# Turned copies of x, positions and taps from the host in a three-block fp32 transformer kernel

## The reference

```python
for l in range(2):
    h = rms_norm(x, pre_g[l])
    p = split_columns(h @ w_in[l] + b_in[l])       # 14 groups of columns, 6992 in all
    # four mixers: stick-breaking, sparse (with compressed blocks), forgetting, latent attention
    # compress_blocks: silu((tokens[:, gather] + pos_emb).reshape(...) @ w1) @ w2
    # latent_attention: rms_norm(c_q) @ w_uq, rms_norm(c_kv) @ w_ukv
    x = x + rms_norm(concat(mixers * silu(gates)) @ w_out[l], post_g[l])
proj = rms_norm(x, norm1_g) @ w_in_2               # banded attentions and a causal conv of 31 taps
x = x + concat(...) @ w_out_2
h2 = rms_norm(x, norm2_g)
x = x + (silu(h2 @ w_gate) * (h2 @ w_up)) @ w_down
```

## Time and profile before

| what | value |
| --- | --- |
| median of the runs | 1979.77 us |
| span of the profiled execution, first to last instruction | 1977.6 us |
| median less span | 2.2 us |
| PE busy | 1963.8 us, 99% of the span |
| DVE, ACT, POOL busy | 58%, 48%, 4% |
| span less PE busy | 13.8 us |
| DMA, whole span | 360.74 MB, mean 182 GB/s |
| DMA in the first two fortieths of the span | 289 and 201 GB/s |

### The profile page before, as it was taken

The page is one execution under the profiler, slowest core; times in us unless marked ns, Lnnn a source line. Parts: engine busy times, 40 slices in busy tenths (PEclk is TensorE's granted clock), DMA queues, the critical chain, the costliest instruction groups (busy, mean ns, idle before and its releaser), DMA issues.

```text
span 1977.6 us, 27533 instructions
## 1 busy us (share of the span) xinstructions
PE 1963.8 (99%) x10170; PEld 1666.5 (84%) x10170; DVE 1145.0 (58%) x1352; ACT 945.6 (48%) x1256; POOL 80.1 (4%) x125
## 2 busy tenths in 40 slices
PE   9999999999999999999999999999999999999999
PEld 7898988887899998888778788888888888888887
DVE  6584555556666554655757986645454444444443
ACT  6355444444564554444655564544444444443342
POOL 4000000001200000000300100000000000000000
PEclk9999999999999999999999999999999999999999
DMA  8664555665755445666555435666666666656653
GB/s 289 201 221 125 165 163 164 191 197 158 251 178 193 145 145 150 194 197 187 168 171 161 143 133 181 193 191 191 191 188 184 190 191 189 189 180 214 205 203 128
DMA packets 188153, 360.74 MB, mean 182 GB/s; under 512 B 13202, under 2 KB 20417, under 8 KB 187793
## 3 DMA queue, kind: packets, MB, share of 16 engines
q1 hardware_dynamic: 183408, 346.15, 56.3%
q0 software_dynamic: 4640, 13.20, 2.4%
HBM read 357.20 MB, written 2.10 MB: 182 GB/s over the span
## 4 chain that ended last, share of the span: by engine, by line
PE 97%; DVE 1%; ACT 1%; DMA 0%; issue 0%; ACTq 0%; POOL 0%; DVEq 0%; SPq 0%; POOLq 0%
PE psum L627 26%; PE psum L629 25%; PE psum L628 25%; PE psum L635 3%; PE psum L638 3%; PE psum L637 3%; PE psum L1334 1%; PE psum L745 1%; PE psum L1110 1%; PE psum L759 1%; PE psum L734 1%; PE psum L891 0%; PE psum L1591 0%; PE psum L653 0%; PE psum L655 0%; PE psum L654 0%
## 5 line engine op out<-in xcount | busy, mean ns | idle before, releaser
L593 DVE TENSOR_TENSOR wl<-raw,wh 128x1024 fp32r<-128x1024 f32 (+1 forms) x655 | 775.4, 1196 | 663.2 <-ACT wh L585 656.0
L585 ACT ACTIVATE wh<-raw 128x1024 fp32r<-128x1024 f32 (+1 forms) x655 | 671.9, 1036 | 826.7 <-PE psum L629 681.8
L627 PE MATMUL psum<-wh,xh 128*128 128x512 f32 (+2 forms) x1584 | 615.5, 389 | 5.0 <-DVE xl L929 4.1
L629 PE MATMUL psum<-wh,xl 128*128 128x512 f32 (+2 forms) x1584 | 608.8, 384 | 0.0
L628 PE MATMUL psum<-wl,xh 128*128 128x512 f32 (+2 forms) x1584 | 608.6, 384 | 0.0
L627 PEld LDWEIGHTS psum<-wh,xh 128*128 128x128 f32 x1584 | 297.6, 188 | 67.0 <-DVE xl L929 7.1
L629 PEld LDWEIGHTS psum<-wh,xl 128*128 128x128 f32 x1584 | 297.5, 188 | 58.7
L628 PEld LDWEIGHTS psum<-wl,xh 128*128 128x128 f32 x1584 | 297.8, 188 | 56.7
L635 PE MATMUL psum<-xh,wh 128*128 128x256 f32 x512 | 146.1, 285 | 0.0
L638 PE MATMUL psum<-xl,wh 128*128 128x256 f32 x512 | 144.9, 283 | 0.0
L637 PE MATMUL psum<-xh,wl 128*128 128x256 f32 x512 | 144.9, 283 | 0.0
(11 more groups left out here) (422 smaller groups left out, 1600.8 us busy)
## 6 DMA issues: line engine op xcount, KB each, us to landing
raw<-in_w_in_dram SPq DMA_DIRECT2D x263, 512.0 KB, 4.3
raw<-in_w_out_dram SPq DMA_DIRECT2D x96, 512.0 KB, 3.9
raw<-in_w_gate_dram SPq DMA_DIRECT2D x88, 512.0 KB, 3.6
raw<-in_w_up_dram SPq DMA_DIRECT2D x88, 512.0 KB, 3.6
raw<-in_w_down_dram SPq DMA_DIRECT2D x80, 512.0 KB, 3.6
cmp_raw<-in_cmp_w_dram SPq DMA_DIRECT2D x16, 512.0 KB, 4.4
raw<-in_w_small_dram SPq DMA_DIRECT2D x16, 336.0 KB, 3.1
bias<-in_b_in_dram POOLq DMA_DIRECT2D x18, 256.0 KB, 4.1
```

Of the source, the lines that this page charges most:

```text
L585: act.activation(wh[:, n % SPLIT_SLOTS, 0:k, 0:unit.n], buffer[:, 0:k, 0:unit.n], ACT.Copy).then_inc(hi_done, 1)
L593: dve.tensor_tensor(out=wl[:, n % SPLIT_SLOTS, 0:k, 0:unit.n], in0=buffer[:, 0:k, 0:unit.n], in1=wh[:, n % SPLIT_SLOTS, 0:k, 0:unit.n].bit ...
L627: pe.matmul(o, ah_[:, kt, tok], hi_w, start=first, stop=False)
L629: ins = pe.matmul(o, al_[:, kt, tok], hi_w, start=False, stop=last)
```

## The change

The host also passes x with columns in partitions (`x_turned`, 128 x 16 x 256), the positions turned (`pos_turned`) and the taps of the conv turned (`conv_w_turned`).

- In layer 0, `xt` takes the turned x (in the place of `ml`); ACT and DVE make the operand from it directly, so the 32 transposes of x in layer 0 go. SP loads `xt` in pieces of two row tiles ahead of each of the first units, and x by tokens (two DMAs of 1 MB) behind raw7 and raw8. The squares of x stand behind the high splits of units 9 and 10, where they stood ahead of those of 6 and 7.
- The gains, the identity and one piece of `xt` are issued by ACT's queue at the very start, where the identity was issued by SP and the gains by POOL.
- DVE takes the operand ahead of the split of each unit, ACT too. The first unit's products are written out in another order, with seven idle products ahead where there were eight and six.
- Positions come by one DMA straight to `posT`; PE's two small transposes and DVE's copy go, in both layers. Taps come straight to `conv_wT`; PE's four small transposes and ACT's copy go in the third block.
- POOL starts its masks when the last piece of `xt` has landed, and issues `w_uq` when seven parts of the operand are done.
- `_out_high` signals of the third block share one semaphore; no instruction moves by that.

```diff
@@ act_first, layer 0
-                act.wait_ge(raw_first, 16)
+                act.wait_ge(xt_first, 16)
+                x_high(0, xt[:, 0, :]).then_inc(first_x_high, 1)
+                act.wait_ge(raw_first, 16)
                 act.activation(wh[:, 0, 0, :], raw[:, 0, 0, :], ACT.Copy).then_inc(first_high, 1)
-                act.wait_ge(s(name + "_turned"), 1)
-                x_high(0, all_banks[:, x_column(0):x_column(0) + T])
-                x_high(1, all_banks[:, x_column(1):x_column(1) + T]).then_inc(s(name + "_high"), 1)
+                act.wait_ge(*xt_signal(0))
+                x_high(1, xt[:, 1, :]).then_inc(s(name + "_high"), 1)
...
-                if n >= 6:
-                    act_norm(name, scratch, updates, n - 6)
+                act_operand(place, name, n)
                 split_high(place, n, units[n])
-                act_operand(place, name, n)
@@ dve_first, layer 0
-                for n in range(2, PARTS):
+                for n in range(1, PARTS):
+                    operand(n)
                     split(n)
-                    operand(n)
@@ SP
+            def load_xt(k0, k1, loaded):
+                sp.dma_start(xt[:, k0:k1, :], d["x_turned"][:, k0:k1, :]).then_inc(loaded, 16)
+            def load_x(tb):
+                sp.dma_start(x[:, tb, :], d["x"][0, tb * P:(tb + 1) * P, :]).then_inc(x_loaded[tb], 16)
...
+                    if l == 0 and n < PARTS:
+                        load_xt(2 * n, 2 * n + 2, xt_loaded[n % XT_SEMS])
+                    load_unit(sp, place, n, layer_units[n], layer_src(l))
+                    if l == 0 and n in (PARTS - 1, PARTS):
+                        load_x(n - PARTS + 1)
@@ POOL
-            load(norm_g, d["norm_gains"][0, :, :], norm_g_loaded)
-            pool.wait_ge(x_loaded[BLOCKS - 1], 16)
+            pool.wait_ge(*xt_signal(PARTS - 1))
...
-                pool.wait_ge(s("pre_turned"), part_signal(place, l, PARTS - 1))
+                if l:
+                    pool.wait_ge(s("pre_turned"), part_turned(place, PARTS - 1))
+                else:
+                    pool.wait_ge(s("pre_operand"), PARTS - 1)
...
-                load(pos_in[0:CMP_LEN, 0, :], mat("nsa_cmp_pos_k"), layer_loads)
-                load(pos_in[0:CMP_LEN, 1, :], mat("nsa_cmp_pos_v"), layer_loads)
+                load(posT[:, :, :], d["pos_turned"][bass.ds(l, 1), :, :, :].rearrange("a p i n -> (a p) i n"),
+                     layer_loads)
@@ PE, first unit and the two small turnings
-            pe_idle_products(8, False)
-            block_0 = pe_turn_block("pre", 0, 0)
-            next(block_0)
-            pe_idle_products(6, False)
+            pe_idle_products(7, False)
+            pe.wait_ge(first_operand, 1)
+            pe.wait_ge(first_high, 1)
...
-                    pe.wait_ge(layer_loads, 16 * LAYER_LOADS * place.once)
-                    for i in range(2):
-                        ins = pe.transpose(st[:, 1024 + 32 * i:1024 + 32 * (i + 1)], pos_in[0:CMP_LEN, i, :],
-                                           ident[0:CMP_LEN, 0:CMP_LEN])
...
-            def turn_conv_weights():
@@ ACT
+            act.dma_start(norm_g, d["norm_gains"][0, :, :]).then_inc(ident_loaded, 16)
+            act.dma_start(ident[:, :], d["c_ident"]).then_inc(ident_loaded, 16)
+            act.dma_start(xt[:, 1:2, :], d["x_turned"][:, 1:2, :]).then_inc(xt_loaded[0], 16)
...
+                if l == 0:
+                    after_unit.update({PARTS + 1 + tb: lambda tb=tb: act_norm("pre", xn, 0, tb) for tb in range(TB)})
```

More of the change, by code:

```diff
@@ L874, in wait_x @@
         def wait_x(eng, name, updates, b):
[L875 to L878, removed]
+            eng.wait_ge(x_ready, BLOCKS * (updates - 1) + b + 1)
         def act_norm(name, scratch, updates, tb):
             act = nc.scalar
-            for b in range(BLOCKS if updates <= LAYERS else 1):
-                wait_x(act, name, updates, b)
+            if updates == 0:
+                act.wait_ge(x_loaded[tb], 16)
+            else:
+                for b in range(BLOCKS if updates <= LAYERS else 1):
+                    wait_x(act, name, updates, b)
             act.activation(scratch[:, :], x[:, tb, :], ACT.Square, accum_out=x_sums[:, tb:tb + 1])
@@ L901, in pe_turn_block @@
         def pe_turn_block(name, updates, b):
[L903 to L907, removed]
+            wait_x(nc.tensor, name, updates, b)
+            for ins in turn_x(range(4 * b, 4 * b + 4), all_banks, x_column(4 * b)):
                 ins.then_inc(s(name + "_turned"), 1)
[L909 to L912, removed]
         def pe_turn_rows(name, updates, tb):
@@ L940, in rows_signal, with xt_signal, turned_before, part_turned @@
             return parts_before(place) + 2 * tb + part + 1
+        def xt_signal(part):
+            return xt_loaded[part % XT_SEMS], 16 * (part // XT_SEMS + 1)
+        def turned_before(place):
+            return (PARTS + 2) * max(place.once - 2, 0)
+        def part_turned(place, part):
+            return turned_before(place) + part + 3
+        def rows_turned(place, tb, part):
+            return turned_before(place) + 2 * tb + part + 1
         def rows_column(kt, tb):
@@ L945, in act_rows_operand @@
         def act_rows_operand(place, name, tb, part):
-            nc.scalar.wait_ge(s(name + "_turned"), rows_signal(place, tb, part))
+            nc.scalar.wait_ge(s(name + "_turned"), rows_turned(place, tb, part))
             for kt in (2 * part, 2 * part + 1):
@@ L1074, in pe_first_operand @@
             if n < PARTS:
-                for b in {3: (2,), 5: (3,)}.get(n, ()):
-                    for _ in pe_turn_block(name, updates, b):
-                        pass
+                if updates and n in (3, 5):
+                    pe_turn_block(name, updates, {3: 2, 5: 3}[n])
                 nc.tensor.wait_ge(s(name + "_operand"), part_signal(place, updates, n))
@@ L1082, in pe_first_units @@
             pe = nc.tensor
-            pe_idle_products(8, False)
-            block_0 = pe_turn_block("pre", 0, 0)
-            next(block_0)
-            pe_idle_products(6, False)
[L1088 to L1098, removed]
-                    pe.wait_ge(lo_done, RAW_SLOTS + 2)
-                else:
-                    for _ in pe_turn_block("pre", 0, 1):
-                        pass
-            multiply(place, 0, units[0], pieces=first)
-            multiply(place, 1, units[1], pieces=second)
+            pe_idle_products(7, False)
+            pe.wait_ge(first_operand, 1)
+            pe.wait_ge(first_high, 1)
+            for tb in range(TB):
+                tok, o = slice(tb * P, (tb + 1) * P), acc[0][:, tb, :]
+                pe.matmul(o, xh[:, 0, tok], wh[:, 0, 0, :], start=True, stop=False)
+                pe.matmul(o, xl[:, 0, tok], wh[:, 0, 0, :], start=False, stop=False)
+            pe.wait_ge(first_low, 1)
+            for tb in range(TB):
+                pe.matmul(acc[0][:, tb, :], xh[:, 0, tb * P:(tb + 1) * P], wl[:, 0, 0, :], start=False, stop=False)
+            pe.wait_ge(s("pre_operand"), 1)
+            pe.wait_ge(lo_done, RAW_SLOTS + 1)
+            for tb in range(TB):
+                tok, o = slice(tb * P, (tb + 1) * P), acc[0][:, tb, :]
+                pe.matmul(o, xh[:, 1, tok], wh[:, 0, 1, :], start=False, stop=False)
+                pe.matmul(o, xh[:, 1, tok], wl[:, 0, 1, :], start=False, stop=False)
+                ins = pe.matmul(o, xl[:, 1, tok], wh[:, 0, 1, :], start=False, stop=False)
+            ins.then_inc(unit_used, 1)
+            pe_first_operand(place, "pre", 1, 0)
+            multiply(place, 1, units[1])
         def pe_turn_mix(o, bank):
@@ L1281, in _ @@
             load(log_count[:, :], d["c_log_count"], block2_loads)
-            pool.wait_ge(s("first2_turned"), part_signal(place, LAYERS, PARTS - 1))
-            load(conv_raw[0:TAPS, :], d["conv_w_2"][0, :, :], block2_loads)
+            pool.wait_ge(s("first2_turned"), part_turned(place, PARTS - 1))
+            load(conv_wT[:, :, :], d["conv_w_turned"], block2_loads)
             pool_norm(place, "first2")
```

96 lines of the change are left out of this document (46 added, 50 removed).

## The result

The changed kernel takes 1984.09 us (median of 15 runs, 1983.26 to 1986.59), the kernel before 1979.84 in the same session: 4.25 us slower, ratio 1.0022, 95% interval 1.0015 to 1.0029. The prediction was 1984.1.

What follows compares the result with a forecast made beforehand. The chain from layer 0's loads to unit 12 was taken to bind: +4.6 us there less 0.35 for the taps gives +4.3, a span of 1981.9, and with 2.2 around it 1984.1 us; range 1979.4 to 1986.4.

Steps and rivals of the forecast that it cites:

- What bounds it: Layer 0: the chain from the layer's loads to unit 12 has only 0.26 us of slack; shifts carry to layer's end.
- What goes from PE: Layer 0: 32 transposes go, unit 1 starts at 11.55, not 12.35; PE alone would gain 4.2 us by stage 2.
- Landing of the loads: Layer 0: POOL's last load lands at 40.3, 4.9 us late; unit 12 +4.6 us.
- served nearly in order of issue: DMA engines: weights issued before w_uq, and the second x at 5.2 us, count as ahead of POOL's loads.
- the two units that I counted: Layer 0 weights: raw11 and raw12 now issued ahead of w_uq, adding 1.3 us each to the landing.
- PE stands idle at units 9 or 10 for raw: Layer 0: a sign, named beforehand, that the forecast is wrong.
- add nothing: ACT, layer 0: squares of x behind unit 10's split cost nothing; they and POOL's factors are done by 38.
- PE's wait: Layer 0: PE idle some 8 us ahead of unit 11, then without a gap from unit 12 at about 52.
- Taps: Third block: turning the taps on the host spares PE four small transposes, a plain gain of 0.35 us.
- Faster: Rival, chance 0.05: chain does not bind, PE's 4.2 us and the taps' 0.35 come through; 1975.2 us.
- Worse: Rival, chance 0.10: raw10 and x land behind POOL's loads, or raw12 and raw13 stand ahead; +5.5 to +7, 1985.3 to 1987.
- The queue yields: Rival, chance 0.28: POOL's loads share the engines with SP's, landing 36.5 to 38.5; +0.5 to +2.5, 1980.3 to 1982.3.

Runs made afterwards that it cites:

- e1: Changed kernel without the two loads of x by tokens (2 MB), POOL filling x with a constant; 1983.76 us, ratio to the kernel before 1.0019.
- e5: Changed kernel without the second x, and with POOL's masks begun at the fourth piece of xt; 1982.62 us, ratio to the kernel before 1.0013.
- e8: Kernel before with only the positions and the taps turned on the host; 1979.24 us, ratio 0.9996.
- e9: Changed kernel without the second x, POOL's masks from the fourth piece of xt, both squares of x behind unit 8; 1978.56 us.
- e12: Changed kernel, all loads kept; layer 0: squares of x behind unit 8, latents read out one split earlier, w_uq's two splits later; 1978.62 us.
- e6: Changed kernel with both squares of x behind unit 8, and SP holding raw 11 and later weights until the layer's loads have landed; 1981.89 us.
- e11: Kernel before plus two more 1 MB loads of x into a free place, behind raw 7 and raw 8; 1985.52 us, ratio 1.0028.
- e10: Changed kernel with squares of x behind unit 8, and w_uq's two splits moved behind the latents' work and a later unit, both layers; 1981.12 us.
- e3: Changed kernel with both squares of x behind the high split of unit 8; 1983.74 us, ratio to the kernel before 1.0020.

## Why the prediction was right, point by point

- *The number.* That it fits to the hundredth is luck. The traced span grew by 3.8 and not by 4.3. In every run 1.7 to 1.9 us lie around the span; the 2.2 that I took from before, and the 2.7 of the changed kernel, hold also by how much the traced execution was quicker than the median, and that made up the half microsecond.
- *What bounds it.* Right: the chain from the layer's loads sets unit 12. Unit 12 +4.34 (forecast +4.6), then no idle time of PE from 55 to 460, and most of the shift stays: +4.04 at PE's longest wait in the seam to layer 1 (486.89 for 482.85).
- *What goes from PE.* Unit 1 at 11.07, forecast 11.55: raw 1 came 0.8 earlier than I took it. Worth nothing, as said.
- *Landing of the loads.* Forecast 40.3, measured 39.9; w_uq issued at 28.05, forecast 28.4, where my own terms (19.6 + 8.5) give 28.1. The number is right, the sum behind it is not sound. "Ahead of it in the DMA engines there is now x a second time: 5.2 us" would have e1 land at about 35; it landed at 39.5, since the ring of weights fills the place. The step that fails is "served nearly in order of issue". Two errors offset: taking x away moved this landing by 0.5 and not by 5.2, and more weights shared its time than the two units that I counted. x had landed at 28.3, just as w_uq was issued; it had pushed back raw 9, 10, 11 and 12, which landed at 32.6, 35.5, 39.5 and 40.9, around posT at 39.9.
- *Raw 9.* I priced x against POOL's loads and not against raw 9, which stands behind it in SP's own queue. I named "PE stands idle at units 9 or 10 for raw" as a sign against me; it came (2.04 us). It stayed hidden since PE had over 4 us in hand, but it held ACT too: the squares ended at 38.73, 1.27 us before L1812. That the squares "add nothing" was nearly false, and e5 shows where it becomes so.
- *PE's wait.* Forecast some 8 us ahead of unit 11; measured 2.04 + 3.84. The rest, 2 us, went into slower products: a stretch at half clock from 36.14 to 39.48, by which units 9 and 10 took 7.4 us and not 5.5. I did not foresee it, nor the second stretch, in unit 11 itself (last section).
- *Small parts.* Taps -0.27 (forecast -0.35: the first product there still starts 0.40 behind the last, not 0.228). Layer 1: nothing, as forecast. Positions in layer 0: in e8 0.38 for unit 12, hidden in the changed kernel.
- *The rivals.* "Faster" (1975.2) had the condition that the last load lands before 31.2. That is not enough: in e9 posT landed at 31.3 (issued at 22.47, 8.8 us), yet L1812 began at 34.99, behind two squares and two splits on ACT, and the time was 1978.6. Nor do the loads alone decide, as e12 shows. "Worse" has a wrong sum at its lower end: squares at 42.7 are 5.2 late, and less the 0.26 of slack and the 0.35 of the taps that is +4.6, inside the forecast, and not +5.5. "The queue yields" is half true as a mechanism (rows of both queues are served together) and wrong in its time.

What stays open: why raw 10 lands at 35.5 in the changed kernel and at 38.1 in e6 with fewer bytes behind it, and whether e8, e9 and e12 are faster than the kernel before. The medians say 0.7 to 1.3 us, the ratios' intervals reach past 1, and in the traces unit 12 of e9 and e12 starts no earlier than before (48.07 and 47.72 for 47.56).

## What to carry to other kernels

When the DMA engines are full, a load that you take away need not give its bytes back at the load that you care about: here a prefetch ring filled the place (in e1 0.5 us came back, of the 5.2 that 2 MB take at 402 GB/s). One that you add can cost all of them (5.1 us in e11). Ask which loads are queued at that moment, on all queues. And before paying with bytes for a faster engine, look for work in the late chain that stands ahead of the wait and need not: here four moves on ACT and DVE gave 5.5 us with every load as it was. Where several waits end within 2 us of each other, as here, single edits can show next to nothing though all of them together show the whole.

## What the hardware showed beyond that

After PE's waits of 2.04 and 3.84 us the granted clock fell to half, 1.2 of 2.4 GHz: the first time 1.1 us into the work that followed (the wait ended at 35.03), the second time with its first product. It stayed there for 3.3 and 3.2 us (windows of the changed kernel, PE alone: stretch, length, busy, clock, DMA share, GB/s):

```profile
36.14:39.48 3.34, 3.34 (x10) 0.51 1.03 404
...
46.24:49.39 3.15, 3.15 (x7) 0.50 0.64 175
```

A product then starts 0.43 us after the last instead of 0.228. Unit 11 took 4.42 us instead of 2.73, and in e1, after a wait of 7.32, and in e5, after 4.42, all of it ran at half clock and took 5.29. In e1 PE reached unit 12 at 52.66 while DVE had split it by 51.3, so the clock cost 1.4 us of the end; in the same way 1.3 us in e5, 0.8 in e10 and 0.7 in e3. So part of what those edits won on ACT and DVE was lost again on PE. The Trainium skill ("TensorE: Matmul & The Clock Gate", section "Part 1: The HAM clock gate (the "warmup" mystery)") names the same two levels, and the trace agrees. In e12, with waits of 2.01 and 1.43, the clock stayed at 1.00, while in e10 it fell after one of 2.02: which waits cost the clock can't be told from these runs.
